# Tiled products, wider moves and moved steps in the state-space part of a one-core encoder layer

## What is computed

```python
xn = rmsnorm(h, norm1_g)
q, k, v, u, gates = split(xn @ w_in)              # 256, 256, 256, 512, 2048 columns
q, k = rmsnorm(q per head), rmsnorm(k per head)   # 4 heads of 64
attn = stick_breaking_attention(q, k, v)
y = s5_ssm(u, ...)                                # 32 groups of 16 inputs, 64 complex states
g = gelu(y); ssm = g * sigmoid(g @ w_glu + b_glu)
h = h + (sigmoid(ga) * (attn @ w_attn_proj) + sigmoid(gs) * (ssm @ w_ssm_proj)) @ w_o
up = causal_dwconv(rmsnorm(h) @ w_up); h = h + (silu(up_g) * up_v) @ w_down
```

## Time and profile before

| | us |
|---|---|
| median of 3 runs (712.18 to 714.67) | 712.98 |
| the profiled execution | 712.44 |
| its span, first to last instruction | 710.7 |
| PE busy | 702.5 |
| DVE / ACT / POOL busy | 415.4 / 319.7 / 187.6 |
| one unit of 48 products of 252 or 264 columns | about 5.8 |

### The profile page before, as it was taken

One profiled execution on the slowest core, in us unless ns is written; L12 is line 12 of the kernel. 1 busy time (PEld: TensorE's weight loads), 2 busy tenths in 40 slices (PEclk: granted clock), 3 DMA queues, 4 the chain that ended last, 5 costly groups with the idle time before them and its releaser, 6 DMA issues.

```text
span 710.7 us, 13993 instructions
## 1 busy us (share of the span) xinstructions
PE 702.5 (99%) x5552; PEld 668.8 (94%) x5552; DVE 415.4 (58%) x557; ACT 319.7 (45%) x474; POOL 187.6 (26%) x215
## 2 busy tenths in 40 slices
PE   8999999999999999999999999999999999999998
PEld 7899899989999999999999999999999998888887
DVE  5764488867787756545765666666666662222221
ACT  4754343558888654435443444443343442211220
POOL 7899999940000022232011010101011010000000
PEclk9999999999999999999999999999999999999999
DMA  8163444545211233333333332323333343333331
GB/s 230 56 201 81 95 126 97 106 96 164 60 33 60 66 90 112 89 90 92 89 99 100 95 89 89 89 89 89 89 98 97 105 121 89 97 96 96 96 97 45
DMA packets 140520, 69.25 MB, mean 97 GB/s; under 512 B 24067, under 2 KB 138471, under 8 KB 140479
## 3 DMA queue, kind: packets, MB, share of 16 engines
q1 hardware_dynamic: 140319, 68.65, 35.0%
q10 hardware_dynamic: 160, 0.02, 0.0%
HBM read 63.19 MB, written 4.28 MB: 95 GB/s over the span
## 4 chain that ended last, share of the span: by engine, by line
PE 90%; DVE 3%; ACT 3%; SPq 1%; issue 1%; DMA 1%; POOL 0%; DVEq 0%; ACTq 0%
PE ps L1803 81%; PE ps L1987 1%; PE ps L2045 1%; PE ps L1854 1%; PE ps L1952 1%; PE ps L2012 1%; ACT xh L982 1%; SPq L626 1%; DMA xtok<-in_x_dram 1%; SPq L533 1%; ACT hi L913 1%; PE ps L1863 1%; PE ps L1921 1%; PE ps L1904 0%; PE ps L1947 0%
## 5 line engine op out<-in xcount | busy, mean ns | idle before, releaser
L1296 DVE TENSOR_TENSOR lo<-raw,hi 128x1024 fp32r<-128x1024 f32 (+2 forms) x102 | 136.5, 1339 | 152.6 <-ACT hi L913 152.3
L1803 PE MATMUL ps<-xh,hi 128*128 128x264 f32 (+1 forms) x1088 | 219.6, 283 | 0.1
L1803 PE MATMUL ps<-xl,hi 128*128 128x264 f32 (+1 forms) x1088 | 218.7, 282 | 0.0
L913 ACT ACTIVATE hi<-raw 128x1024 fp32r<-128x1024 f32 (+2 forms) x102 | 111.5, 1093 | 237.1 <-PE ps L1803 232.3
L1803 PE MATMUL ps<-xh,lo 128*128 128x264 f32 (+1 forms) x1088 | 217.9, 282 | 0.0
L1803 PEld LDWEIGHTS ps<-xh,hi 128*128 128x128 f32 x1088 | 167.2, 189 | 1.7 <-issue 0.8
L1803 PEld LDWEIGHTS ps<-xl,hi 128*128 128x128 f32 x1088 | 166.7, 188 | 0.0
L1803 PEld LDWEIGHTS ps<-xh,lo 128*128 128x128 f32 x1088 | 166.7, 188 | 0.0
L896 POOL TENSOR_TENSOR cv<-cv 128x512 f32<-128x512 f32 x22 | 28.4, 1289 | 226.7 <-DVE cv L1755 226.7
L1803 PE MATMUL ps<-ah,hi 128*128 128x512 f32 (+1 forms) x198 | 74.3, 375 | 0.0
L1803 PE MATMUL ps<-al,hi 128*128 128x512 f32 (+1 forms) x198 | 73.1, 369 | 0.0
(11 more groups left out here) (291 smaller groups left out, 966.1 us busy)
## 6 DMA issues: line engine op xcount, KB each, us to landing
raw<-in_w_up_dram SPq DMA_DIRECT2D x88, 256.0 KB, 3.1
raw<-in_w_in_dram SPq DMA_DIRECT2D x52, 256.0 KB, 3.4
raw<-in_w_down_dram SPq DMA_DIRECT2D x16, 384.0 KB, 3.3
raw<-in_w_down_dram SPq DMA_DIRECT2D x16, 320.0 KB, 4.0
raw<-in_w_o_dram SPq DMA_DIRECT2D x16, 256.0 KB, 2.9
xtok<-in_x_dram SPq DMA_DIRECT2D x4, 512.0 KB, 5.7
raw<-in_w_ssm_proj_dram SPq DMA_DIRECT2D x8, 256.0 KB, 2.9
out_dram<-yt SPq DMA_DIRECT2D x7, 256.0 KB, 2.4
```

Of the source, the lines that this page charges most:

```text
L913: act.activation(hi[slot][:, 0:n * P], raw[slot][:, 0:n * P], ACT.Copy)\
L1296: dve.tensor_tensor(lo[slot][:, 0:n * P], raw[slot][:, 0:n * P], hi[slot][:, 0:n * P].bitcast(F32), ALU.subtract)\
L1803: ins = pe.matmul(o, weights[w], acts(a, c), start=start and i == 0, stop=stop and i == 2)
```

## The change

1. **Taps on two tiles.** `prep(r)` on PE writes taps of even pairs to output rows 0 to 47 and of odd pairs to 64 to 111 in turn, in two column blocks. ACT copies them in four pieces of 256 columns, not in two of 512.
2. **Readout on four tiles.** Each of the 16 `xst` products of a round becomes two, of 64 output rows each: 32 products on four combinations of contraction half and output half.
3. **Norms.** Each of the four tiles of squares is summed into 32 output rows of its own (0, 32, 64, 96). ACT takes the sums out with eps; four DMAs write them to `sum_dram`, one reads them back as 128x33; ACT (`rates`) and DVE (Newton step) work on 128x33; one DMA writes, and two spread them.
4. **Maps.** DVE forms part c = 0 of the output maps of all four rounds (units 6, 7, 8 and 12), where POOL formed it for rounds 0 and 1. POOL forms only c = 1.
5. **Moves.** `u_read` reads two rounds at a time (16 groups a DMA, all in place by unit 6, `uc` holds four rounds). `y_write` is one DMA a round instead of eight, `y_read` eight instead of one.
6. **V** is turned in three pieces, in one bank, behind units 10, 12 and 14 rather than two behind 12 and 14; the ten transposes are the same.
7. **Heads 0 and 1** are split as steps of their own: head 0 behind unit 15, head 1 behind unit 16 ahead of `readout(3)`.
8. **Masks** in `scores` stand ahead of the products of their bank.

```diff
-         5: [("square", 0)], 6: [("square", 1)],
-         7: [("square", 2)], 8: [("square", 3), ("prep", 0)], 9: [("state", 0), ("norms", 0)],
-         10: [("prep", 1), ("out_map", 2)], 11: [("readout", 0), ("state", 1)],
-         12: [("prep", 2), ("turn_v", 0), ("out_map", 3)] + [("scale", i) for i in range(4)], 13: [("readout", 1), ("state", 2)],
-         14: [("prep", 3), ("turn_v", 1)], 15: [("readout", 2), ("state", 3)],
-         16: [("readout", 3)],
+         5: [("square", 0)], 6: [("square", 1), ("out_map", 0)],
+         7: [("square", 2), ("out_map", 1)], 8: [("square", 3), ("out_map", 2), ("prep", 0)],
+         9: [("state", 0), ("norms", 0)],
+         10: [("prep", 1), ("turn_v", 0), ("rates", 0)], 11: [("readout", 0), ("state", 1)],
+         12: [("prep", 2), ("turn_v", 1), ("out_map", 3)] + [("scale", i) for i in range(4)], 13: [("readout", 1), ("state", 2)],
+         14: [("prep", 3), ("turn_v", 2)], 15: [("readout", 2), ("state", 3), ("head", 0)],
+         16: [("head", 1), ("readout", 3)],
...
+         7: [("rms_write", 0)], 8: [("rms_read", 0)], 9: [("norm_write", 0), ("toep", 0)],
+         10: [("norm_read", 0)], 11: [("rate_write", 0), ("rate_read", 0)],
...
             def norms(_):
                 pe.wait_ge(sq_ready, 4)
-                rows = slice(0, NORM_ROWS[1] + 4)
                 for c in range(2):
                     for i in range(4):
-                        w = HL if norm_of(i)[0] else HLL
-                        ins = pe.matmul(ps[rows, 6 + c, 0:w], sel[:, i], sq[i][:, c * w:(c + 1) * w],
-                                        start=i == 0, stop=i == 3, skip_group_check=True)
+                        c0 = c * (HL if norm_of(i)[0] else HLL)
+                        ins = pe.matmul(ps[NORM_TILE * i:NORM_TILE * (i + 1), 6 + c, 0:HL],
+                                        sel[:, i], sq[i][:, c0:c0 + HL],
+                                        start=True, stop=True)
...
-                if r >= 2:
-                    pe.wait_ge(h_dve, r - 1)
-                for i in range(RP):
+                pe.wait_ge(h_dve, r + 1)
+                for k in range(RP // 2):
                     for c in range(2):
-                        ins = pe.matmul(ps[0:3 * GH, 6, i * P:(i + 1) * P],
-                                        bpair[:, c, r * RP + i, :],
...
+                        for half in range(2):
+                            i = 2 * k + half
+                            p0 = ST * half
+                            ins = pe.matmul(ps[p0:p0 + 3 * GH, 6, k * P:(k + 1) * P],
+                                            bpair[:, c, r * RP + i, :],
...
                 for c in range(2):
                     for g in range(2 * RP):
                         part = slice(ST * (g % 2), ST * (g % 2) + ST)
-                        ins = pe.matmul(group_out(g), hout[r % HOUTS][part, c, g // 2, 1:T8 + 1, :]
-                                        .rearrange("p i h -> p (i h)"),
-                                        xst[part, c, g // 2, :], start=False, stop=c == 1,
-                                        skip_group_check=True)
+                        maps = hout[r % HOUTS][part, c, g // 2, 1:T8 + 1, :]\
+                            .rearrange("p i h -> p (i h)")
+                        for half in range(2):
+                            mine = slice(ST * half, ST * half + ST)
+                            ins = pe.matmul(group_out(g)[mine], maps[:, mine],
+                                            xst[part, c, g // 2, :], start=False, stop=c == 1,
+                                            skip_group_check=True)
...
+                if r == 0:
+                    dve.wait_ge(pw_set, 1)
+                    for u in u_out:
+                        dve.wait_ge(u, 16)
                 map_part(dve, link, r, 0, mod_flat)
...
-            output_map(0, (0, 1))
+            output_map(0)
...
-            output_map(1, (0, 1))
+            output_map(1)
```

More of the change, by code:

```diff
@@ L124 @@
 GLU_BANKS = (2, 0, 6, 4)
-NORM_ROWS = (0, 32)
-TURN_BANK = (4, 4)
+NORM_TILE = 32
+TURN_BANK = 7
 HOUTS = 3
@@ L212, in hybrid_trunk @@
         sq = [gates[:, 16 * LL - (i + 1) * L:16 * LL - i * L] for i in range(4)]
-        row_v, row_r, row_t = (sq[i][0:2 * NORM_ROWS[1], :] for i in range(3))
+        sq_all = gates[:, 16 * LL - 4 * L:16 * LL]
+        row_v = sq[0]
         hout_end = 16 * LL - 4 * L
@@ L289, in hybrid_trunk @@
         lal = alloc(heads, "lal", [P, SUM_COLS], F32R)
+        ql2 = [alloc(heads, f"ql2{i}", [P, LL], F32R) for i in range(2)]
         k2 = [alloc(heads, f"k2{i}", [P, L], F32R) for i in range(2)]
@@ L369, in hybrid_trunk @@
         u_out = [sem(f"u_out{i}") for i in range(ROUNDS)]
-        u_in = [sem(f"u_in{i}") for i in range(ROUNDS)]
+        u_in = [sem(f"u_in{i}") for i in range(2)]
         y_out = [sem(f"y_out{i}") for i in range(ROUNDS)]
@@ L386, in hybrid_trunk @@
         rows_set = sem("rows_set")
-        norm_out = sem("norm_out")
-        norm_in = [sem(f"norm_in{i}") for i in range(4)]
+        sum_out = sem("sum_out")
+        sum_in = sem("sum_in")
+        rate_out = sem("rate_out")
+        rate_in = sem("rate_in")
         kh_set = sem("kh_set")
@@ L989, in squares @@
                 act.wait_ge(drained, unit + 1)
+                if not is_k:
+                    act.activation(sq[i][:, LL:L], qT[:, t, 0:LATE0], ACT.Square)
                 act.activation(sq[i][:, 0:w], (kT if is_k else qT)[:, t, 0:w], ACT.Square)\
@@ L1126, in gelu @@
                         .then_inc(gh_set, 1)
-            steps = {"square": squares, "norms": norms, "prep": prep, "readout": readout, "turns": turns,
-                     "scores": scores,
+            steps = {"square": squares, "norms": norms, "rates": rates, "prep": prep, "readout": readout, "turns": turns,
+                     "head": head, "scores": scores,
                      "suffix": suffix, "values": values, "gelu": gelu, "turn_v": turn_v}
@@ L1662, in _ @@
             steps = {"columns": columns, "out_map": out_map, "angle": angle, "turns": turns,
-                     "norms": norms, "scale": scale, "prep": prep, "state": state,
-                     "readout": readout,
+                     "rates": rates, "scale": scale, "prep": prep, "state": state,
+                     "head": head,
                      "scores": scores, "suffix": suffix, "values": values, "gelu": gelu,
@@ L2058, in run @@
                     pe.wait_ge(masks_set, 4)
-                bank = {"turn_v": TURN_BANK}.get(name, (0,) * 4)[i]
-                if bank == 4 or name in ("prep", "state", "scores") or (name, i) == ("columns", 0):
+                if name in ("prep", "state", "scores") or (name, i) == ("columns", 0):
                     for s_, n in used45 if name != "scores" else ():
```

238 lines of the change are left out of this document (126 added, 112 removed).

## The result

The changed kernel took 715.88 us (714.71 to 716.79) against 712.98 for the kernel before: a ratio of 1.0034, with an interval from 1.0020 to 1.0048. It is slower by about 2.9 us and not faster by 9. The profiled execution took 716.25 us with a span of 714.5, 3.8 more than before.

The account below looks back on a forecast made before the run. The prediction took PE as the bound, busy 702.5 of 710.7 us. Its terms, 3.7 + 2.6 + 3.3 + 0.4 + 0.45 - 0.7 - 0.8 = 8.95, gave 703.8 us against 712.98, range 700.5 to 708.5.

Parts of the forecast that it names:

- Taps, norms, readouts, masks: PE's products: taps on two tiles save 3.7 us, norms 2.6, readouts on four tiles 3.3, grouped masks 0.4.
- the rule that the prediction gives from the Trainium skill: On PE, a weight load overlaps products in flight only when the row group differs; the prediction already saw the trace disagree.
- the third rival: On PE, loads don't run under the other half's products, so readouts, taps and norms lose: 722.2 us, chance 0.03.
- SP "costed at nothing": In SP, taps' DMAs and unit 12's load queue behind norm_write's wait; with 15 us and more between, no cost.
- DVE's new maps, "nothing on PE": Three operations of some 1.1 us each in DVE's passes 6 to 8, idle 4.1 us a unit: no cost.
- POOL's run beside state(3), -0.8: At readout(3): 2.3 us more of state(3) beside POOL's run over hT, costing 0.8 us; bounds -1.6 and +1.2.
- Prep(3), -0.7: PE waits 0.9 to 1.0 us at prep(3) for POOL's map and DVE's state(2), against 0.3: 0.7 us lost.
- Suffix(0), 0.45: Heads split earlier free ACT and DVE at unit 17, so suffix(0) becomes as long as suffix(1): 0.45 us saved.
- its four faster outcomes: Whole kernel: forecast 0.50, tiles two at a time 0.23, POOL and DVE bound 0.13, no wait left 0.07.
- Its signs of being wrong: A unit's product waits for lo between units 8 and 17, taps stay at 1.88, or something past unit 20 changes length.
- "POOL and DVE become the bound": DVE's denser work slows POOL by 5% on 50 us: 2.5 us at prep(3), 0.8 at state(3); 707.2, chance 0.13.

Follow-up runs that it names:

- kernel 1: Changed kernel with norm_write moved behind the load of unit 12 in SP, nothing else: 713.5 us, 1.0002.
- kernel 11: Changed kernel with norm_write behind the load of unit 12 and rate_read behind unit 14's load and round 1's taps; POOL's run unmoved: 705.8 us, 0.9898.
- kernels 3: Changed kernel with norm_write behind the load of unit 12 and POOL's run over hT held until state(3) is done: 706.4 us, 0.9898.
- kernel 5: Changed kernel with norm_write behind unit 12's load, rate_read behind unit 14's load and round 1's taps, POOL's run over hT behind state(3): 704.6 us.
- kernel 13: kernel 5 with toep(0) also moved behind the load of unit 12 in SP: 704.0 us, 0.9876.
- kernel 9: kernel 5 with POOL's run over hT held until head 0's values are summed: 711.4 us, 0.9980.
- kernel 10: kernel 5 with POOL's run over hT held until the values of all four heads are summed: 714.3 us, 1.0012.
- kernel 12: The kernel before with POOL's run over hT held until state(3) is done, nothing else: 716.65 us, 1.0049.
- (2): Changed kernel with only POOL's run over hT held until DVE has finished state(3): 710.0 us, 0.9957.
- kernel 4: The kernel before with only taps on two tiles, xst products on four and masks first: 714.3 us, 1.001.
- (8): Changed kernel with V alone undone, turned in two pieces behind units 12 and 14 in banks 4 and 5: 714.0 us, 1.001.
- kernel 7: kernel 5 with the maps undone, POOL again forming both parts of the output maps of rounds 0 and 1: 708.1 us, 0.9935.

## Why the prediction was wrong

- *Taps, norms, readouts, masks.* Right. 3.7 predicted and 3.5 measured; 2.6 and 2.6; 3.3 and 3.3 at full clock (`xst` 1.1 us, as predicted); masks 0.4 and 0.5 (the scores of head 0 went from 2.09 to 1.99 us, those of heads 1 to 3 from 2.19 to 2.06). Four tiles do run at once: 64 records in 1.10 us, 17 ns each, against 60. Loads run under the other tiles' products, so the taps at 63 ns a record disagree once more with the rule that the prediction gives from the Trainium skill, "TensorE: Matmul & The Clock Gate", Part 3 (The mechanism), and the third rival, at 722.2, is out by its mechanism too.
- *SP "costed at nothing".* This is the step that failed. It saw rightly that `norm_write` waits till about 86 us (87.8 measured) with the load of unit 12 behind it, but measured the cover to the wrong consumer: PE's product of unit 12, "15 us and more". The first consumer is ACT's split of that unit, ready at 93.5; from the load's landing (5.2 us after its issue) that leaves an issue at 88. It was issued at 94.7, 6.3 us of wait on ACT, of which 3.4 reach PE through the steps queued behind the split. With `norm_write` moved it is issued at 90.5 (kernel 1): the other 2 us of lateness are `toep(0)`'s. The same held for `rate_read` ahead of unit 14 (2.2 us of wait on ACT), which the prediction did not price at all, and which brought more once `norm_write` was mended: 7.7 of the 10.1 us with POOL's run where the change has it (kernels 1 and 11), at most 1.8 with the run moved (kernels 3 and 5). The two orders in SP alone take 10 us off (715.9 to 705.8).
- *DVE's new maps, "nothing on PE".* Wrong by the same path: a map ahead of kern(0) holds `toep(0)` in SP and so the load, and with `toep(0)` behind the load ACT's wait is gone (kernel 13). What it costs in time is within the spread.
- *POOL's run beside state(3), -0.8.* The mechanism was right, the place and the price were not. POOL keeps its own time (start 132.8), so when PE and DVE came late, state(2) slid under the run. The price was put at a third of a microsecond for each beside it; measured are 13.0 - 5.8 = 7.2 us for 12.5, 0.58. In kernel 11, where the late loads are mostly mended, 1.5 us of wait stand ahead of each of readout(2) and readout(3), 3.0 in all, where the prediction had 2.0 ahead of the second alone.
- *Prep(3), -0.7.* A wait of 1.3 for `mod` instead of 1.0: near in number, but for another reason, since DVE's chain came late behind the loads; in kernel 11 it is 0.3. POOL's side was right: input map 3 ends at 127.8, 50 us after input map 1 starts, against 126.3.
- *Missing: the clock.* The prediction took every wait at its length. With waits of 2.4 us and more the granted clock fell to its lower level in thirteen of fifteen cases, which in the changed kernel cost 1.5 and 2.0 us more. And 1.6 us of slow start lie in this profile. For the kernel before, no trace shows a slow start; a few of its runs have a mean clock of 0.995 to 0.997, most have 0.999 or 1.000.
- *Suffix(0), 0.45.* 1.51 us against 1.68: 0.17 saved.
- *Small slips of the sum.* 712.98 less 8.95 is 704.0 and not 703.9 or 703.8, and its four faster outcomes add up to 0.93 where it says 0.90.
- *Its signs of being wrong.* None of the three appeared: no product of a unit waited for `lo`, the taps took 1.01 us, and from 231 us on all lies 3.8 us later than before, up to the end. The loss came in through steps between the units, which no sign watched.
- *The rivals.* "POOL and DVE become the bound" named the right engines at 5%, far too mild. None put a load behind a moved wait. With SP's orders mended the change gives 705.8 us, and 704.0 to 704.6 with POOL's run moved as well: so the forecast of 703.8 is near what the changed work is worth with its side work in a fit order. That it is this near is in part luck: POOL's run had to be moved for it, which the change does not do, and the terms for POOL's run and suffix(0) did not come out.

What stays open: what makes the slow start come or not, and why two waits of 2.4 and 3.1 us left the clock alone (below).

## What to carry to other kernels

When a wait goes into a queue that also issues loads, look for the first consumer of each load behind it, here a split on another engine, and for what stands behind that consumer, not for the product that uses the data. When PE gets shorter, work of other engines that keeps its own time slides over other steps: say for each long run which chain lies under it at the new times, and cut it into pieces that fit that chain's idle time. Price a long wait on PE (here 2.4 us and more) by what follows at half clock as well.

## What the runs showed of the hardware

- *A run on POOL costs DVE by the operation, not by a share of bandwidth*: 1.66 to 1.76 us instead of 0.68 to 0.71 for operations with two SBUF inputs in state(2), nothing for one whose other input is in PSUM. DVE's rows in head 1, first beside the run in kernel 9 and then without it in kernel 5, show two things more:

```profile
177.60 1.08 DVE L1599 COPY later<-aw 128x128 f32<-128x128 f32 x1
179.91 1.30 DVE L1601 TENSOR_TENSOR later<-aw 128x16 f32<-128x16 f32 x1
182.63 1.35 DVE L1603 CAST lah<-later 128x416 fp32r<-128x416 f32 x1
...
180.41 0.23 DVE L1599 COPY later<-aw 128x128 f32<-128x128 f32 x1
180.69 0.17 DVE L1601 TENSOR_TENSOR later<-aw 128x16 f32<-128x16 f32 x1
181.23 0.38 DVE L1603 CAST lah<-later 128x416 fp32r<-128x416 f32 x1
```

The size does not matter: 16 columns, which take 0.17 us alone, take 1.30, about the length of one of POOL's operations there (1.3 us). A copy or cast with one SBUF input is held up as well; no trace shows in which mode it runs. One operation of state(2), line 1544, slipped through at 0.47 us instead of 0.43. So a chain of small operations loses most: the five from line 1599 on take 6.4 us instead of 1.2. One run cost PE 4.7 (10.4 us long, kernel 9), 6.1 (16.8, kernel 10) or 2.6 us (12.6, kernel 12); four pieces of 2.6 to 3.6 us nearly nothing, but they also lie largely where DVE has nothing of the chain to do.
- *Half clock after idle time.* PE's waits of 3.4 and 5.3 us (changed kernel), 2.4 and 3.8 (kernel 1), 2.9 (2), 3.5 (3), 2.8 (4), 2.6 and 4.2 (8), 4.7 (9), 2.9 and 6.1 (10) and 2.6 (12) were each followed by some microseconds at 0.50, at once or a microsecond later. A wait of 2.4 in kernel 4 (155 us) and one of 3.1 in kernel 7 were not, the latter with PE all but idle here:

```profile
91.00:94.00 3.00, 0.34 (x3) 0.13 (x2) 2.90 (x4) 0.60 (x1) 2.76 (x4) 1.00 0.61 180
94.00:96.00 2.00, 1.58 (x18) 1.44 (x20) 2.00 (x3) 1.54 (x2) 1.70 (x3) 1.00 0.07 9
```

So the length of the wait does not decide it alone. What the lower level costs where it comes is 1.5 and 2.0 us in the changed kernel and more where PE goes on busily behind the wait: kernel 4's stretch lasts from 113 to 120 us. Waits up to 1.5 us (kernels 11 and 13) were not followed by it.
- *Four 64x64 tiles* take 64 records with their loads in 1.10 us, the same in both rounds at full clock.
